# An encoder layer with expert choice: the two sample halves chosen in one joint list, the router on rows ahead of their norm, and two weight units ahead at the first expert

## The reference

```python
def rms_norm(x, g):
    y = xf * lax.rsqrt(jnp.mean(xf * xf, axis=-1, keepdims=True) + EPS)
    return (y * g).astype(x.dtype)

def expert_choice_ffn(h, w_router, w_gate, w_up, w_down):
    cap = max(1, EC_CAPACITY * n_tok // N_EXPERTS)        # 128 rows (sample), 64 (prompt)
    aff = jax.nn.softmax((flat @ w_router).astype(jnp.float32), axis=-1)
    g, idx = lax.top_k(aff.T, cap)                        # each of 16 experts picks its rows
    xs = flat[idx]
    hid = jax.nn.silu(xs @ w_gate) * (xs @ w_up)          # per expert
    out = (hid @ w_down) * g[..., None]
    y = jnp.zeros(...).at[idx].add(out)

x = x + mixer(rms_norm(x, g_mix), ...)                    # ends in "... @ w_out"
h = rms_norm(x, norm_ffn_g)
x = x + expert_choice_ffn(h, ...)
return rms_norm(x, final_norm_g)
```

## Time and profile before

| | |
|---|---|
| median of 3 runs | 2129.41 us |
| profiled execution | 2129.28 us, span 2127.4 us |
| PE busy | 1995.8 us (94% of the span) |
| DVE busy | 1431.3 us (67%) |
| ACT busy | 1105.3 us (52%) |
| POOL busy | 352.8 us (17%) |
| granted TensorE clock, mean | 0.978 of full speed |
| mixer's last product to the first expert's product | 1152.55 to 1210.64 us of the span |

### The profile page before, as it was taken

The page is one execution under the profiler, slowest core; times in us unless marked ns, Lnnn a source line. Parts: engine busy times, 40 slices in busy tenths (PEclk is TensorE's granted clock), DMA queues, the critical chain, the costliest instruction groups (busy, mean ns, idle before and its releaser), DMA issues. The chain is left out here.

```text
span 2127.4 us, 43417 instructions
## 1 busy us (share of the span) xinstructions
PE 1995.8 (94%) x16136; PEld 1756.0 (83%) x16136; DVE 1431.3 (67%) x2481; ACT 1105.3 (52%) x1959; POOL 352.8 (17%) x499
## 2 busy tenths in 40 slices
PE   7999998999999998897998499999999999999996
PEld 6887886788878776776887499999999999999995
DVE  5457457667675667576278577777777777778885
ACT  5322222566666333564232266666666766667774
POOL 1213213000000332001221101111111111111234
PEclk9999999999999999999999699999999999999998
DMA  5211101000021222212322468878888787888995
GB/s 186 80 37 38 31 27 41 26 21 20 21 75 44 61 70 67 64 45 88 121 108 90 164 215 269 252 255 253 256 253 261 250 262 248 263 261 293 347 328 186
DMA packets 183465, 317.82 MB, mean 149 GB/s; under 512 B 11872, under 2 KB 82016, under 8 KB 183328
## 3 DMA queue, kind: packets, MB, share of 16 engines
q1 hardware_dynamic: 169984, 281.06, 39.3%
q0 software_dynamic: 8608, 30.68, 5.8%
q10 hardware_dynamic: 4736, 4.19, 0.6%
HBM read 279.97 MB, written 35.91 MB: 148 GB/s over the span
## 5 line engine op out<-in xcount | busy, mean ns | idle before, releaser
L2360 DVE TENSOR_TENSOR we_lo<-raw,we_hi 128x1024 fp32r<-128x1024 f32 x384 | 466.0, 1223 | 204.2 <-ACT we_hi L2285 203.2
L2251 PE MATMUL psum<-x_parts,we_hi 128*128 128x384 f32 x2048 | 586.4, 360 | 3.7 <-DVE x_parts L2367 3.7
L2253 PE MATMUL psum<-x_parts,we_lo 128*128 128x192 f32 x2048 | 514.0, 251 | 0.0
L2285 ACT CAST we_hi<-raw 128x1024 fp32r<-128x1024 f32 x384 | 400.3, 1054 | 187.8 <-PE psum L2253 95.9
L2253 PEld LDWEIGHTS psum<-x_parts,we_lo 128*128 128x128 f32 x2048 | 392.8, 192 | 0.6
L2251 PEld LDWEIGHTS psum<-x_parts,we_hi 128*128 128x128 f32 x2048 | 385.9, 188 | 4.5 <-DVE x_parts L2367 4.0
L613 PE MATMUL psum<-hT_hi,w_hi 128*128 128x512 f32 x512 | 210.5, 411 | 0.7 <-issue 0.7
L615 PE MATMUL psum<-hT_hi,w_lo 128*128 128x512 f32 x512 | 201.1, 393 | 0.0
L614 PE MATMUL psum<-hT_lo,w_hi 128*128 128x512 f32 x512 | 200.7, 392 | 0.0
L134 POOL TENSOR_TENSOR carried_pool<-minus_half 128x1 f32<-128x1 f32 x47 | 17.4, 370 | 635.6 <-ACT result_s L2327 488.7
L615 PEld LDWEIGHTS psum<-hT_hi,w_lo 128*128 128x128 f32 x512 | 96.6, 189 | 21.4
(11 more groups left out here) (334 smaller groups left out, 3955.8 us busy)
## 6 DMA issues: line engine op xcount, KB each, us to landing
raw<-in_w_gate SPq DMA_DIRECT2D x128, 512.0 KB, 4.7
raw<-in_w_up SPq DMA_DIRECT2D x128, 512.0 KB, 6.6
raw<-in_w_down SPq DMA_DIRECT2D x128, 512.0 KB, 5.2
w_raw<-in_w_in SPq DMA_DIRECT2D x96, 256.0 KB, 2.8
y_rows<-x SPq DMA_DIRECT2D x12, 512.0 KB, 2.6
h_rows<-h SPq DMA_DIRECT2D x12, 512.0 KB, 2.9
y<-y_rows SPq DMA_DIRECT2D x12, 512.0 KB, 8.0
w_raw_s<-in_w_in SPq DMA_DIRECT2D x16, 256.0 KB, 3.0
```

The lines of the kernel that those rows point to most:

```text
L2251: pe.matmul(out[:, 0:2 * SLOTS], w_hi[:, s, at], x_parts[p][:, k, :, :], start=(k == 0), stop=False, skip_group_check=True)
L2253: mm = pe.matmul(out[:, SLOTS:2 * SLOTS], w_lo[:, s, at], x_hi[p][:, k, :], start=False, stop=(k == DT - 1), skip_group_check=True)
L2285: act.copy(w_hi[:, n % PARTS, :], raw[:, s, :]).then_inc(hi.sem, 1)
L2360: dve.tensor_tensor(w_lo[:, n % PARTS, :], raw[:, n % RAW, :], w_hi[:, n % PARTS, :].bitcast(F32), ALU.subtract).then_inc(lo.sem, 1)
```

## The change

It has five parts.

1. **The choice.** Halves one and two of the sample stand in neighbouring groups of partitions (0, 32, 64 in place of 0, 96, 64), and one instruction works on both (48 partitions, later 80 with the prompt's first table). 70 instructions in place of 120. They can begin only when all eight sample tiles are placed, so they stand in tiles 8 to 11, and less of the joint table is left behind the last tile. The last replacements, whose result nobody reads, are dropped.
2. **The router.** `turn` reads x1 instead of h2, so it needs no norm. The norm's weight g is multiplied into the router once (POOL, `weighted`), and a row's scale is applied in the exponential (`scale=rstd`), its maximum being scaled by one more small DVE instruction (`scaled`). Norm 11 moves behind the last tile.
3. **The order of a tile.** `turn`, `top`, `route` and `place` of tile t-1 stand between the sums of tile t: sum 0, turn, sum 1, router, sum 2, place, sum 3. Before it was sums 0 and 1, place t-2, turn t-1, sums 2 and 3, and the router behind them. The split numbered 2t+2 stays first in the list of tile t.
4. **The merge.** The first merge is split between DVE and POOL, and its columns are taken at the very end.
5. **The first expert.** Two units of weights (`AHEAD`) instead of three are loaded and split ahead of the gathered rows; PE issues 16 dummies behind the first turn; a product of unit 0 waits only for its own quarter of x_parts.

```diff
-GROUPS = [0, 96, 64]
+GROUPS = [0, 32, 64]
@@ Rounds
-        joint = [(both, table[both, :], r * TOP) for r in range(of_s - of_p, of_s)]
+        paired = [(pair, table[pair, :], r * TOP) for r in range(of_s - of_p)]
+        joint = [(every, table[every, :], r * TOP) for r in range(of_s - of_p, of_s)]
...
+        steps[1].pop()
+        steps[2].pop()
@@ project_out, the list of steps
+    SCORED = {FIRST_TILE: (2, 1, 5, 3), FIRST_TILE + 1: (2, 1, 5, 4), FIRST_TILE + 2: (2, 1, 5, 4), NT - 1: (2, 1, 3, 4)}
...
-            tiles += [("sum", t, 0), ("sum", t, 1)]
-        if t >= 2:
-            tiles.append(("place", t - 2))
-        if t:
-            tiles.append(("turn", t - 1))
+            tiles.append(("sum", t, 0))
...
+        tiles += [("turn", n) for n in scored]
         if t < NT:
-            tiles += [("sum", t, 2), ("sum", t, 3), ("rows", t)]
+            tiles.append(("sum", t, 1))
...
+        tiles += [step for n in scored for step in (("top", n), ("route", n))]
+        if t < NT:
+            tiles.append(("sum", t, 2))
...
+        tiles += [("place", n) for n in scored]
+        tiles += choose(behind[3])
@@ behind the tiles
+    tiles += [*left, ("back", 0), *choose(3), ("merge", 0), *choose(6), ("norm", NT - 1), *choices, ("merge", 1)]
@@ PE, turn and top
-                pe.wait_ge(normed, t + 1)
+                if t == NT - 1:
+                    pe.wait_ge(added, 2 * (NT - 1))
+                    keep_clock(pe, SUMS[NT % 2][0], ident, 14)
+                pe.wait_ge(added, 2 * t + 2)
...
+                if t == NT - 1:
+                    keep_clock(pe, SUMS[NT % 2][0], ident, 8)
-                if t == NT - 2:
-                    pe.wait_ge(added, 2 * (NT - 1))
-                    keep_clock(pe, SUMS[NT % 2][0], ident, 16)
@@ experts
+    AHEAD = 2
...
-            for n in range(PARTS - 1):
+            for n in range(AHEAD):
                 body("split", 0, 0, n)
-            body("turn", 0, 0)
+            body("turn", 0, 0, "first")
+            for n in range(AHEAD, PARTS - 1):
+                body("split", 0, 0, n)
...
-                            if p == 0 and n == PARTS - 1:
+                            if p == 0 and n == AHEAD:
                                 sp.wait_ge(gathered.sem, gathered.at(0, 31))
...
+                        if n == "first":
+                            keep_clock(pe, half(0, "up")[0], ident, 16)
```

More of the change, by code:

```diff
@@ L150, in __init__ @@
         rows = lambda first, end: slice(GROUPS[first], GROUPS[end] + EXPERTS)
-        one, two, three, both = rows(0, 0), rows(1, 1), rows(2, 2), rows(2, 1)
+        pair, every, three = rows(0, 1), rows(0, 2), rows(2, 2)
         of_s, of_p = CAP_SAMPLE // TOP, CAP_PROMPT // TOP
-        first = [(one, table[one, :], r * TOP) for r in range(of_s)]
-        second = [(two, table[two, :], r * TOP) for r in range(of_s - of_p)]
-        joint = [(both, table[both, :], r * TOP) for r in range(of_s - of_p, of_s)]
+        paired = [(pair, table[pair, :], r * TOP) for r in range(of_s - of_p)]
+        joint = [(every, table[every, :], r * TOP) for r in range(of_s - of_p, of_s)]
         last = [(three, table_last[three, :], r * TOP) for r in range(of_p)]
[L157 to L160, removed]
+        steps = [[(*group, what) for group in groups for what in range(3)] for groups in (paired, joint, last)]
+        steps[1].pop()
+        steps[2].pop()
+        self.steps = sum(steps, [])
+        counts = [len(group) for group in steps]
+        self.ends = [sum(counts[:n + 1]) for n in range(3)]
+        self.placed_before = dict(zip([0, *self.ends], (2 * BC, 2 * BC + 2, 3 * BC)))
     def step(self, dve, n):
@@ L1759, in project_out @@
         if t < NT:
[L1760 to L1763, removed]
+            tiles += [("square", t), *choose(behind[0]), ("mean", t), *choose(behind[1])]
+            if t < NT - 1:
+                tiles.append(("norm", t))
+            tiles += choose(behind[2])
     tiles = [step for step in tiles if not any(step in steps for steps in beside.values())]
[L1765 to L1769, removed]
+    left = choose(joint - sum(map(sum, SCORED.values())))
+    tiles += [*left, ("back", 0), *choose(3), ("merge", 0), *choose(6), ("norm", NT - 1), *choices, ("merge", 1)]
     def load(sp, n):
@@ L1984, in body @@
                 chosen.step(dve, t)
-            elif kind == "merge":
+            elif kind == "merge" and t == 0:
                 dve.wait_ge(backed, 4)
[L1987 to L1995, removed]
-                dve.scalar_tensor_tensor(apart[at], back_index[at], float(before), index_f[at], ALU.add,
-                                         ALU.subtract).then_inc(merged, 1)
-                for to in results:
-                    dve.tensor_tensor(best[to], first, second, ALU.max).then_inc(merged, 1)
-                dve.wait_ge(merged, done + 2)
-                dve.tensor_tensor(apart[at], apart[at], later[at], ALU.mult).then_inc(merged, 1)
-                done += 3 + len(results)
-                dve.wait_ge(merged, done)
```

117 lines of the change are left out of this document (83 added, 34 removed).

## The result

| | before | after |
|---|---|---|
| median | 2129.01 us (4 runs, 2128.07 to 2131.05) | 2147.52 us (4 runs, 2145.28 to 2149.64) |
| ratio | | 1.0085, 95% interval 1.0068 to 1.0103 |
| profiled execution | 2129.28 us, span 2127.4 | 2145.28 us, span 2143.5 |

The account below looks back on a forecast made before the run. PE, busy 94% of the span, bounds the kernel, with DVE's choice bounding the tail. Terms -6.4 + 15.0 - 12.85 - 1.4 - 3.0 = -8.65 took 2129.28 to 2120.6 us; forecast's own range 2114 to 2126, overall range 2113 to 2129.

Parts of the forecast that it names:

- start of the tiles: Tile 2: PE starts sum 0 without waiting for norm 0; -6.4 us, bounds -8 and -1.6.
- the wait in tiles 3 to 10: PE idles 1.87 us ahead of each router, for ACT's copies queued behind a split; eight times, +15.0 us.
- the tail: Last sum to last columns: 26.6 us in place of 39.45, mostly 16 joint steps fewer; -12.85 us, bounds -15 and -10.
- landing of the first rows: First expert: 0.5 MB less weight traffic beside the gathered rows lands them sooner; -1.4 us, bounds 0 and -1.6.
- first units at full clock: First expert: the first units run at 2.4 GHz, halving 6.36 us at clock 0.50; -3.0 us, bounds 0 and -3.2.
- the clock in the tiles: Tiles 3 to 10: the forecast let the clock hold through the new waits, at no cost.
- rival C: The new stalls take the clock down once per tile, 8 x 4.8 = 38 us, so 2159 us; chance 7%.
- The load of g_cols: Loading g_cols for the weighted router was cost at nothing, since PE is far behind it.
- DVE keeping up: Tiles 8 to 11: DVE's work, about 13.4 of 15.6 us, delays no rows; cost 0, at most +2 us.
- Rival A: ACT has the turned rows copied before sum 1 ends, so no stall in the tiles; 2105.6 us, chance 7%.
- rival B: Tile 2's 2.7 us wait drops the clock, and the first expert runs at half speed; 2128.4 us, chance 12%.
- never idle: First expert: 16 dummies behind the turn keep PE busy, so the first units run at 2.4 GHz; -3.0 us.

Follow-up runs that it names:

- experiments 1 and 2: Changed kernel with split 2t+2 moved behind the turn, 2116.29 us; changed kernel with seven dummy matmuls between sum 1 and router, 2131.31 us.
- experiment 2: Changed kernel with seven dummy matmuls between sum 1 and the router in tiles 3 to 10, ACT's order left; 2131.31 us.
- experiment 6: The kernel before with an unused buffer of 32 bytes on each partition behind the router, no instruction changed; 2137.54 us.
- experiment 11: kernel 8 with the first eight rounds of the choice on one sample half at a time, 24 more DVE steps; 2126.77 us.
- kernel 8: Changed kernel with both mends: the split numbered 2t+2 behind the turn, and g_cols allocated last; 2108.08 us, ratio 0.9905 to the kernel before.
- experiment 4: Changed kernel with five dummy matmuls between sum 1 and the router in tiles 3 to 10; 2139.6 us.
- experiment 3: Changed kernel with three dummy matmuls between sum 1 and the router in tiles 3 to 10; 2144.55 us.
- Experiment 10: kernel 8 without the 16 dummy matmuls behind the first turn; 2105.37 us.

## Why the prediction was wrong

By its own steps, read in the trace of the changed kernel against that of before:

| term | forecast | measured |
|---|---|---|
| start of the tiles | -6.4 | -6.1 (place 1 at 1028.04, against 1028.77 and 5.4 of shift) |
| the wait in tiles 3 to 10 | +15.0 | +15.4 (experiments 1 and 2) |
| the tail | -12.85 | -13.5 (25.98 against 39.45) |
| landing of the first rows | -1.4 | +0.2 in this execution, -1.0 in the mean |
| first units at full clock | -3.0 | -3.2 |
| the clock in the tiles | 0 | +15.6 |
| the 32 bytes | 0 | +5.4 up to the tiles, +1.6 in them |

The measured terms make +15.4; the spans of the two profiled executions differ by 16.1. The medians differ by 18.5; the other 2.4 us lie in executions that were not traced, and stay open. The 5.4 is the first mixer product of the stretch (`normed`, 1008.11 against 1002.69), the 1.6 nine tiles of 13.97 in place of 13.79.

- **The step that failed** is the rejection of rival C, by which the clock in the tiles was put at nothing: "Against it: the 1.00 in 968 to 972 us, where PE was busy only 1.55 of 4 us". The runs show 15.6 us there. The row was read rightly, but it was one execution, and its stretch ends at 972.00, ahead of the matmul at 972.29 that ends the gap. In the tiles the clock fell 1.1 to 2.8 us behind the stall, so a stretch that ends with the gap can't show such a fall (in that trace there was none: 1.00 from 972 to 980 us). The same gap of 2.63 to 2.65 us stands in all fourteen traces, and the clock fell at it or right behind it in eight of them. In seven the first matmul already takes 0.77 us in place of 0.47; in the eighth, the kernel before with the 32 bytes, it takes 0.47 and the fall comes 1.1 us later. No kernel was traced twice, so whether this changes from one execution to the next, or from one kernel to another, isn't told apart. Here is the gap in experiment 2, to be held against the row of 972.29 in the earlier trace rows, and the fall in the trace of experiment 6:

```profile
977.20 0.77 PE L1844 MATMUL psum<-wo_late_hi,w_hi 128*128 128x512 f32 x1 [2.64 <-issue]
```

```profile
982.36:985.77 3.41, 3.41 (x10) 2.52 (x9) 1.20 (x3) 0.81 (x2) 0.52 (x1) 0.50 0.28 111
```

- The price of rival C was wrong too, and on the other side. It took 4.8 us from the one drop behind 5.23 us of idle. That drop lasted 13.65 us (0.50 from 1005.48 to 1019.13), those in the tiles 3.41 us, at times 6.83: a fall costs 1.55 us, at times 3.15, and eight cost 15.6 in place of 38. Against the kernel without the 32 bytes, 2139.7 us, the rival's 2159 was as far off as the forecast (19.3 and 19.1). With the bursts of the Trainium skill ("TensorE: Matmul & The Clock Gate", section "HAM oscillation — how this bites in real kernels") the trace agrees in this: a wait for data that returns costs the clock each time, eight times of eight at 1.68 us. It differs in where, since the page's bursts start slow and here the fall came 1.1 to 2.8 us behind the wait. At 0.57 us it was six of eight.
- **What was missed.** "The load of g_cols" was cost at nothing, and by the sum of the terms its DMA and the product cost nothing that can be seen. Its place in memory cost 7.8 us. No rival named it, since the argument went by instructions and queues, and the address of a buffer is neither.
- **What held.** The wait, its cause and its size, its absence in tile 11; the tail, though its steps were priced at 0.77 there and at 0.68 in the expectation of experiment 11; DVE keeping up. Rival A, the wait not there, said 2105.6; kernel 8, in which it isn't, took 2108.08.
- **Luck at the start of the tiles.** That term came out to 0.3 us because the clock held behind the wait ahead of router 0, which rival B doubted. Eleven traces have such a wait, 1.76 to 2.33 us; the clock held in two (the changed kernel's and experiment 4's) and fell behind it in nine. Between the turns of tiles 0 and 2, with the same order of work, it is 19.19 us in the changed kernel and 22.28 in experiment 3, where it fell. Router 0 in the two, in that order, each time behind 2.27 us:

```profile
1017.85 1.93 PE L1872 MATMUL psum<-router,h2T 128*128 128x16 f32 x16 [2.27 <-issue]
```

```profile
1019.67 3.57 PE L1874 MATMUL psum<-router,h2T 128*128 128x16 f32 x16 [2.27 <-issue]
```

- **A reason that was wrong behind a term that was right.** The full clock at the first units was put down to PE being "never idle" behind the 16 dummies. Experiment 10 doesn't bear it out: without them the clock is 1.00 too, and the kernel takes 2.7 us less.

With both repaired the change is a gain of 20.4 us (kernel 8). 31.2 us for the place of one entry in a list and 7.8 for the place of one buffer turn it into the loss of 18.5.

## What to carry to other kernels

When a step is moved to where an engine's partner is always busy, look at what stands ahead of it in the partner's own order: a wait there that was harmless becomes one of the whole pipeline. A gap that returns in a dense stream of matmuls should be priced with a fall of the clock as well, even where it is short. A single row that shows no fall proves little: look at the clock for some microseconds behind the gap, and in more than one trace, before it carries a forecast. A small new buffer goes at the end of the allocation, or is padded to 64 bytes, and unchanged stages are compared first (their means, and the start of a landmark behind them) before the changed one is read.

## What the runs showed of the hardware

- Matmuls with fp32r operands and 512 columns took 395 ns in place of 391 and 414 in place of 411 when the buffers behind the router were moved by 32 bytes on each partition; moved by 64 bytes they took 391 and 412. Over the kernel that is 7.8 to 8.7 us, 0.4%. It is the operand with the 512 columns (hT) that moved; the stationary one (w_hi, w_lo) is allocated ahead of the router and stayed, and its loads took 187 to 189 ns, moved or not. Why 32 bytes slow it was not tried.
- Once in each tile, an idle stretch of 0.57 us took the clock down in six tiles of eight, one of 1.01 or 1.68 us in eight of eight, and some 0.1 us in none (one trace each, three with 1.68). A single one of 2.63 to 2.65 us in the attention did in eight traces of fourteen, and one of 1.76 to 2.33 us at the start of the tiles in nine of eleven. What makes the difference between one gap and the next was not tried.
- An instruction of the choice over 512 columns costs the same on 16, 48 and 80 partitions: for MAX8 682, 692 and 690 ns (the kernel before and experiment 11), and 0.77 us from one step to the next on 48 as on the mostly 80 of experiment 11 (18.6 us for 24).
